# Mamba-2 decays of a hybrid decoder from two-part running sums on 32-row groups, with the first round placed ahead of the recurrence's output

## The reference, cut to what matters

```python
dt = softplus(dt_raw + dt_bias)
a = -jnp.exp(a_log)
a_dt = dt * a                                   # 8 heads, 256 tokens, never positive
a_cum = jnp.cumsum(a_dt, axis=-1)
seg = a_cum[..., :, None] - a_cum[..., None, :]
lmat = masked_exp(seg, _causal_mask(ln))        # exp of the segment sums, causal
cb = jnp.einsum('bclgn,bcsgn->bgcls', cc, bc)   # 2 groups
y_diag = jnp.einsum('bgecls,bcsgep->bclgep', cb[:, :, None] * lmat, xc)
```

## Time and profile before

| | us |
|---|---|
| median of 3 runs (lowest, highest) | 1519.15 (1518.85, 1520.54) |
| the profiled execution's own time | 1520.9 |
| its span, first to last instruction | 1518.6 |
| PE busy | 1480.4 (97%) |
| DVE busy | 1176.1 (77%) |
| ACT busy | 938.8 (62%) |
| POOL busy | 51.5 (3%) |

### The profile page before, as it was taken

One profiled execution on the slowest core, in us unless ns is written; L12 is line 12 of the kernel. 1 busy time (PEld: TensorE's weight loads), 2 busy tenths in 40 slices (PEclk: granted clock), 3 DMA queues, 4 the chain that ended last, 5 costly groups with the idle time before them and its releaser, 6 DMA issues.

```text
span 1518.6 us, 21694 instructions
## 1 busy us (share of the span) xinstructions
PE 1480.4 (97%) x8411; PEld 1288.3 (85%) x8411; DVE 1176.1 (77%) x1143; ACT 938.8 (62%) x952; POOL 51.5 (3%) x58
## 2 busy tenths in 40 slices
PE   8999999999999999999999999999999999999996
PEld 8989898999889989897888887888878888888884
DVE  6886654555447887656998998989989899898996
ACT  6655444444437654454777778777777777777773
POOL 0031000000000121000000000000000000000000
PEclk9999999999999999999999999999999999999998
DMA  7433443455546432534699998999889999999993
GB/s 307 142 137 112 149 157 139 143 191 181 185 167 219 140 112 96 185 136 166 248 361 383 346 351 343 352 378 359 342 343 351 377 362 341 361 353 373 365 361 123
DMA packets 54484, 388.51 MB, mean 256 GB/s; under 512 B 6000, under 2 KB 6256, under 8 KB 8176
## 3 DMA queue, kind: packets, MB, share of 16 engines
q1 hardware_dynamic: 53840, 384.98, 67.6%
q10 hardware_dynamic: 544, 2.10, 0.3%
HBM read 386.00 MB, written 1.05 MB: 255 GB/s over the span
## 4 chain that ended last, share of the span: by engine, by line
issue 53%; PE 44%; DVE 2%; DMA 0%; ACT 0%; POOL 0%; DVEq 0%; POOLq 0%
PE pb L1027 12%; PE pb L1029 12%; PE pb L1028 12%; PE pb L1168 1%; PE pb L1246 1%; PE pb L1266 1%; PE pb L1008 1%; DVE xTl L1589 0%; PE pb L1212 0%; DMA h<-in_x 0%; PE pb L1256 0%; PE pb L1222 0%; PE pb L1214 0%; PE pb L1223 0%; PE pb L1213 0%
## 5 line engine op out<-in xcount | busy, mean ns | idle before, releaser
L2105 DVE TENSOR_TENSOR wlo<-raw,whi 128x2048 fp32r<-128x2048 f32 x175 | 400.5, 2291 | 50.5 <-ACT whi L939 48.6
L939 ACT ACTIVATE whi<-raw 128x2048 fp32r<-128x2048 f32 x175 | 335.8, 1919 | 134.7 <-PE pb L1029 134.7
L1540 DVE TENSOR_TENSOR wlo<-raw,whi 128x2048 fp32r<-128x2048 f32 (+1 forms) x101 | 225.7, 2246 | 132.3 <-ACT whi L592 131.9
L1027 PE MATMUL pb<-whi,mTh 128*128 128x512 f32 x768 | 305.0, 397 | 4.9 <-DVE kvXr L2105 3.7
L1029 PE MATMUL pb<-whi,mTl 128*128 128x512 f32 x768 | 300.1, 391 | 0.0
L592 ACT ACTIVATE whi<-raw 128x2048 fp32r<-128x2048 f32 (+1 forms) x101 | 190.1, 1884 | 176.8 <-PE pb L1029 167.6
L1027 PE MATMUL pb<-xTh,whi 128*128 128x256 f32 x736 | 210.0, 285 | 2.0 <-DVE xTl L1577 1.2
L2105 DVE TENSOR_TENSOR kvXr<-kvX,whi 128x2048 fp32r<-128x2048 f32 x86 | 196.7, 2291 | 19.3 <-ACT whi L939 17.8
L1028 PE MATMUL pb<-xTl,whi 128*128 128x256 f32 x736 | 208.2, 283 | 0.0
L1029 PE MATMUL pb<-xTh,wlo 128*128 128x256 f32 x736 | 208.2, 283 | 0.0
L1028 PE MATMUL pb<-wlo,mTh 128*128 128x512 f32 x528 | 205.6, 389 | 0.0
(11 more groups left out here) (330 smaller groups left out, 2220.7 us busy)
## 6 DMA issues: line engine op xcount, KB each, us to landing
raw<-in_ffn_w SPq DMA_DIRECT2D x209, 1024.0 KB, 4.8
kvX<-in_ffn_w SPq DMA_DIRECT2D x88, 1024.0 KB, 4.9
raw<-in_lin_w SPq DMA_DIRECT2D x64, 1024.0 KB, 4.7
raw<-in_lin_w SPq DMA_DIRECT2D x4, 536.0 KB, 5.2
arena<-in_mem ACTq DMA_DIRECT2D x2, 1024.0 KB, 7.8
h<-in_x SPq DMA_DIRECT2D x1, 1024.0 KB, 5.1
out<-xn SPq DMA_DIRECT2D x2, 512.0 KB, 2.7
consts<-in_con SPq DMA_DIRECT2D x1, 836.0 KB, 12.8
```

What stands on the lines that cost most here:

```text
L939: nc.scalar.activation(whi[:, (MOE0 + c) % HRING, :], xraw_slots[c % XRING], ACT.Copy).then_inc(hi_ready, 1)
L1027: nc.tensor.matmul(o, lh, rh, start=first, stop=False)
L1540: V.tensor_tensor(wlo[:, m % RING, c], raw[:, m % RING, c], whi[:, m % HRING, c].bitcast(F32), ALU.subtract).then_inc(lo_ready, 1)
L2105: V.tensor_tensor(xlo_slots[c % XRING], xraw_slots[c % XRING], whi[:, (MOE0 + c) % HRING, :].bitcast(F32), ALU.subtract).then_inc(lo_ready, 1)
```

## The change

- **Running sums instead of masks.** DVE no longer builds `ABm` and `ALm`. Behind the fox maxima it cuts each token's decay into two parts, a coarse one (rounded by adding and subtracting 3072) and the rest, and writes them into columns 32 i to 32 i + 3 of `Wm`, for head i of a round. PE multiplies `Wm` with two triangular masks behind the fox transposes (four matmuls of 128 columns, bank 7): these are the sums towards the border of the two tiles. ACT makes `Qm` and `Km` of them, in which each 32-row group holds four rows in use (coarse, one, rest, one, with signs), and PE waits for them ahead of the fox output.
- **Rounds.** The segment sums of a head are then `Km` times `Qm` on the 32 rows of that head: one matmul of 256 columns and one of 128, with the four heads of a round in four row groups and four banks. DVE clamps the own-tile blocks at zero in PSUM (`nonpositive`) ahead of the exponential.
- **Order.** Round one moves ahead of the recurrence's output, which goes to the second bank of z in place of bank 7; z's activation on ACT moves ahead of the convolution's, so that this bank is free. Its exponential follows (`decays(0)`) before xk0 is copied. The B-C products now wait for that exponential in place of the recurrence's copy. xk1(0) moves ahead of round two, and xk1(1) waits for the recurrence's copy.
- **DVE's order.** The heads' squares come ahead of the B-C product; `xcd` ahead of the splits of chunks 17 and 18; then the product of round one, the clamp of round two, the split of chunk 19, and the product of round two. `ytmp` moves behind the heads' output.

```diff
+COARSE = 3.0 * 2.0 ** 10
...
+             np.concatenate([row[0] - row[2], row[1] + row[3], row[3] - row[1], row[0] + row[2]], axis=1)]
...
-        Mm = carve(8736, M2_H, 3 * P)
+        Mm = [carve(at, 4, 3 * P) for at in (14368, 8736)]
...
-        ALm = carve(14368, NT, M2_H, P)
-        ABm = carve(2560, M2_H, P)
+        Wm = carve(9760, NT, 2, P)
+        Km = carve(2560, 2, S)
+        Qm = carve(3072, 2, S)
...
+                act.wait_ge(m2_c, layer + 1)
+                units = [const("units")[:, i:i + 1] for i in range(4)]
+                sums = pb[:, 7, :].rearrange("p (r s) -> p r s", r=2)
+                nc.scalar.activation(Qm, sums, ACT.Identity, scale=units[0], bias=units[1])
+                nc.scalar.activation(Km, sums, ACT.Identity, scale=units[2], bias=units[3]).then_inc(m2_rows, 1)
...
+                projected(act, "z", layer)
+                b = bank("z", layer)
+                nc.scalar.activation(zs, pb[:, b:b + 2, 0:512], ACT.Silu).then_inc(lin_act, 1)
                 act.wait_ge(conv_ready, layer + 1)
                 nc.scalar.activation(xcv, xcv, ACT.Silu).then_inc(xcv_ready, 1)
-                take("z", layer, (zs, 0, 512, ACT.Silu, 1.0, None))
-                split_to(last_chunk(layer, "xk0") + 2)
+                after("z", layer)
+
+                def decays(r):
+
+                    act.wait_ge(m2_neg, 2 * layer + r + 1)
+                    nc.scalar.activation(Mm[r], pb[:, 4:8, 0:3 * P], ACT.Exp).then_inc(m2_e, 1)
+
+                decays(0)
+                take("xk0", layer, (tiles(kX[:, 0:4, :]), 0, 512, ACT.Copy, 1.0, None))
                 act.wait_ge(m2_t, layer + 1)
                 nc.scalar.activation(xs, pb[:, 6:8, :], ACT.Copy).then_inc(m2_xs, 1)
-                take("xk0", layer, (tiles(kX[:, 0:4, :]), 0, 512, ACT.Copy, 1.0, None))
-                for r in range(2):
-                    act.wait_ge(m2_seg, 2 * layer + r + 1)
-                    nc.scalar.activation(Mm[:, 4 * r:4 * r + 4, :], pb[:, 4:8, 0:3 * P], ACT.Exp).then_inc(m2_e, 1)
-                    if r == 1:
-                        split_to(chunk0(layer, "xk1") + HRING)
+                decays(1)
+                split_to(chunk0(layer, "xk1") + HRING)
                 take("xk1", layer, (tiles(kX[:, 4:8, :]), 0, 512, ACT.Copy, 1.0, None))
...
                 mm.then_inc(fox_pt, 1)
+                pe.wait_ge(m2_w, layer + 1)
+                for rnd in range(2):
+                    o = pb[:, 7, rnd * S:(rnd + 1) * S]
+                    nc.tensor.matmul(o[:, 0:P], Wm[:, 0, rnd, :], const("after"), start=True, stop=True)
+                    mm = nc.tensor.matmul(o[:, P:S], Wm[:, 1, rnd, :], upto, start=True, stop=True)
+                mm.then_inc(m2_c, 1)
...
+                pe.wait_ge(m2_rows, layer + 1)
                 pe.wait_ge(fox_ptc, layer + 1)
...
                 project("xk0", layer, M, (0,))
+                def segments(rnd):
+
+                    for i in range(4):
+                        r = slice(32 * i, 32 * i + 32)
+                        nc.tensor.matmul(pb[:, 4 + i, 0:2 * P], Km[r, rnd, 0:P], Qm[r, rnd, :], start=True, stop=True)
+                    for i in range(4):
+                        r = slice(32 * i, 32 * i + 32)
+                        mm = nc.tensor.matmul(pb[:, 4 + i, 2 * P:3 * P], Km[r, rnd, P:S], Qm[r, rnd, P:S], start=True,
+                                              stop=True)
+                    mm.then_inc(m2_seg, 1)
+
                 pe.wait_ge(hg_sel, (layer + 1) * (MASKED + 1))
                 pe.wait_ge(hg_wide, (layer + 1) * len(WIDE))
+                segments(0)
+                pe.wait_ge(lin_act, evac_count(("z", layer)))
                 for hd in range(HG_H):
                     v = vtok[:, :, 256 + hd * DH:256 + (hd + 1) * DH]
                     at = 4 * (hd % 2) + 2 * (hd // 2)
-                    o = pb[:, 7, :].rearrange("p (t h d) -> p t h d", t=NT, h=HG_H)
+                    o = pb[:, bank("z", layer) + 1, :].rearrange("p (t h d) -> p t h d", t=NT, h=HG_H)
                     nc.tensor.matmul(o[:, 0, hd, :], ScT[:, at, :], v[:, 0, :], start=True, stop=True)
                     nc.tensor.matmul(o[:, 1, hd, :], ScO[:, at // 2, :], v[:, 0, :], start=True, stop=False)
...
                 pe.wait_ge(xcv_ready, layer + 1)
-                pe.wait_ge(hg_ok, layer + 1)
+                pe.wait_ge(m2_e, 2 * layer + 1)
...
                 mm.then_inc(m2_t, 1)
-                pe.wait_ge(m2_a, layer + 1)
+                project("xk1", layer, M, (0,))
                 pe.wait_ge(m2_cb, layer + 1)
                 pe.wait_ge(m2_xs, layer + 1)
-                for rnd in range(2):
-                    if rnd:
-                        project("xk1", layer, M, (0,))
-                        pe.wait_ge(m2_e, 2 * layer + 1)
-                    for i in range(4):
-                        hd = 4 * rnd + i
-                        b = pb[:, 4 + i, :]
-                        nc.tensor.matmul(b[:, 0:2 * P], ALm[:, 0, hd, :], upto_ones, start=True, stop=False)
-                        nc.tensor.matmul(b[:, P:2 * P], ABm[:, hd, :], upto, start=False, stop=True)
-                        mm = nc.tensor.matmul(b[:, 2 * P:3 * P], ALm[:, 1, hd, :], upto, start=True, stop=True)
-                    mm.then_inc(m2_seg, 1)
+                segments(1)
+                pe.wait_ge(hg_ok, layer + 1)
                 project("xk1", layer, M, (1,))
                 pe.wait_ge(m2_m, 2 * layer + 2)
...
+                def pairs(ap):
+
+                    return ap.rearrange("p (r i) -> p r i", r=2).unsqueeze(3).to_broadcast([P, 2, 4, 2])
+
+                for t in range(NT):
+                    ins = V.tensor_scalar(Z12[:, t, 4:12], A12[:, t, 4:12], 2.0 * t - 1.0, COARSE, ALU.mult, ALU.add)
+                link(ins)
+                for t in range(NT):
+                    at = Wm[:, t, :, :].rearrange("p r (i x) -> p r i x", x=32)
+                    V.tensor_scalar(at[:, :, :, 0:2], pairs(Z12[:, t, 4:12]), -COARSE, None, ALU.add)
+                    ins = V.scalar_tensor_tensor(out=at[:, :, :, 2:4], in0=pairs(Z12[:, t, 4:12]), scalar=-COARSE,
+                                                 in1=pairs(A12[:, t, 4:12]), op0=ALU.add,
+                                                 op1=ALU.subtract if t else ALU.add)
+                ins.then_inc(m2_w, 1)
...
 
-                V.tensor_copy(ABm, bc(A12[:, 1, 4:12], P))
-                for t in range(NT):
-                    ins = V.tensor_tensor(ALm[:, t, :, :], const("after").unsqueeze(1).to_broadcast([P, M2_H, P]),
-                                          bc(A12[:, t, 4:12], P), ALU.mult)
-                ins.then_inc(m2_a, 1)
+                def nonpositive(rnd):
+
+                    dve.wait_ge(m2_seg, 2 * layer + rnd + 1)
+                    own = pb[:, 4:8, 0:3 * P].rearrange("p b (i s) -> p b i s", i=3)[:, :, 0:3:2, :]
+                    V.tensor_scalar(own, own, 0.0, None, ALU.min).then_inc(m2_neg, 1)
+
+                nonpositive(0)
                 dve.wait_ge(hg_o, layer + 1)
-                V.tensor_copy(xn[:, :, 256:512], pb[:, 7, :].rearrange("p (t c) -> p t c", t=NT)).then_inc(hg_ok, 1)
+                V.tensor_copy(xn[:, :, 256:512], pb[:, bank("z", layer) + 1, :].rearrange("p (t c) -> p t c", t=NT)
+                              ).then_inc(hg_ok, 1)
 
                 ss = ssq.rearrange("p (t c) -> p t c", c=10)
                 rs = rstd.rearrange("p (t c) -> p t c", c=10)
                 heads = xn[:, :, 0:512]
                 after("z", layer)
-                dve.wait_ge(m2_t, layer + 1)
-                V.tensor_tensor(CBs, pb[:, 4:6, 0:3 * P], const("m2mask").unsqueeze(1).to_broadcast([P, 2, 3 * P]),
-                                ALU.mult).then_inc(m2_cb, 1)
-                after("xk0", layer)
-                dve.wait_ge(m2_xs, layer + 1)
-                for t in range(NT):
-                    tokens = xs[:, t, :].rearrange("p (h d) -> p h d", d=DH)
-                    V.tensor_tensor(xcd[:, t, :].rearrange("p (h d) -> p h d", d=DH), tokens, bc(SP12[:, t, 4:12], DH),
-                                    ALU.mult)
-                    V.tensor_tensor(ytmp[:, t, :].rearrange("p (h d) -> p h d", d=DH), tokens,
-                                    bc(par_("m2_d", layer), DH), ALU.mult)
                 dve.wait_ge(hg_ok, layer + 1)
                 link(V.tensor_tensor(sqh, heads, heads, ALU.mult))
                 link(V.tensor_reduce(ss[:, :, 0:8], sqh.rearrange("p t (h d) -> p t h d", d=DH), AX.X, ALU.add))
                 V.tensor_scalar(ss[:, :, 0:8], ss[:, :, 0:8], 1.0 / DH, EPS, ALU.mult, ALU.add).then_inc(ss_ready, 1)
+                dve.wait_ge(m2_t, layer + 1)
+                V.tensor_tensor(CBs, pb[:, 4:6, 0:3 * P], const("m2mask").unsqueeze(1).to_broadcast([P, 2, 3 * P]),
+                                ALU.mult).then_inc(m2_cb, 1)
+                def by_heads(ap, t):
+
```

(43 more changed lines are left out.)

## The result

The changed kernel takes 1531.91 us (median of 4, 1531.35 to 1535.77) against 1519.02 (1518.85 to 1520.54): a ratio of 1.0082, 95% interval 1.0070 to 1.0094. It is 12.9 us slower, where 1.0 us slower, 1520.2, was forecast and 1524.2 was the top of the range.

The account below looks back on a forecast made before the run. TensorE (PE), busy 97% of the span, was taken to bound the kernel. Work at -0.5 us plus a clock loss of 1.5 gave +1.0 on the median 1519.15: 1520.2, range 1515.8 to 1524.2.

Parts of the forecast that it names:

- PE's work: PE's sums and rounds: 0.88 and two of 1.1 added, 6.93 and a 1.20 wait removed; 5.05 us shorter per layer.
- rival 2: Segment-sum rounds on PE: 32-row groups run one after another, 3.0 us a round, 1523.9 in all; chance 0.17.
- The chain to y: From xk0(1)'s end through ACT and DVE: y starts 19.9 us later, PE idles about 5, work gives -0.5 us.
- rival 3: Round two's clamp in PSUM on DVE costs 2.4 us, +3.4 in all, 1522.5; chance 0.10.
- Edits at nothing: Small DVE weight steps, ACT's passes over the sums, and round one's clamp and exp: all covered, costing nothing.
- Rival 1: Before y: chunk 19's split is not in the way, PE idles 0.8 us, 9 us faster, 1510; chance 0.10.
- The clock: Half clock after the idle before y: 0.75 us per layer, 1.5 in all, bounds 0 and 1.7 per layer.
- The dip agrees: Claim that the earlier trace's mid-run clock dip, priced at 1.7 us, supports the skill's advice against long idle gaps.
- the sum: Whole kernel: -0.5 for the work plus 1.5 for the clock, +1.0 us, 1520.2 against the median.

Follow-up runs that it names:

- experiment 1: Changed kernel with DVE's split of chunk 19 put back behind the product of round two: 1515.29 us, ratio 0.9963 to the kernel before.
- experiment 8: Changed kernel with round two's clamp ahead of round one's product and chunk 19's split behind both products: 1508.94 us, ratio 0.9928 to the kernel before.
- experiment 5: Changed kernel, idle kept, with the wide product xv0(0) moved ahead of y behind the same wait: 1537.63 us.
- experiments 3 to 7: DVE squarings added: kernel before 1543.81, experiment 8 1527.69; changed kernel with xv0(0) before y 1537.63, extra matmuls before y, wide 1530.61, narrow 1543.00 us.

## Why the prediction was wrong

- **PE's work:** right. Forecast 0.88 for the sums, 1.1 for a round, 5.05 us per layer in all; measured 0.91, 0.87 and 5.42 (0.91 + 1.06 - 4.95 - 2.44 = -5.42, where 1.06 is round one with the changes of form around it). The four row groups ran at once, so rival 2 is out. 12 units of 0.219 in a row are 2.63, and 2.63 / 0.87 = 3.0. The Trainium skill's 3.07 for four 32-row tiles ("TensorE: Matmul & The Clock Gate", section on packing small matmuls) agrees.
- **The chain to y:** right. Forecast 19.9 us behind xk0(1) and an idle of about 5; measured 602.33 - 582.46 = 19.87 and 4.97. The split of chunk 19 was the cause (experiment 1). The clamp took 1.23 against the 1.21 of the earlier trace rows; rival 3 is out.
- **Edits at nothing:** the small DVE steps, ACT's two passes and the early round brought no wait of PE in the new stage; of PE's waits only y's is new there. The 2.09 us at 30.7 us lie ahead of everything that the change touches in a layer.
- **Rival 1** (faster, 1510) did not happen, and was what experiment 8 then made: 1508.9.
- **The clock: the step that failed.** "I take half, 0.75 per layer, 1.5 in all, bounds 0 and 1.7 per layer." Measured 6.1 and 7.5, 13.6 in all. The price came from the earlier trace rows, one dip of 3.4 us with matmuls of 256 columns behind it, and I took its length over as it was. (Half of 1.7 is also 0.85 and not 0.75; that is 0.2 in all and changes nothing.) The length depends on what follows. Behind y's idle stand 24 products of 64 columns, and the dip lasts 13.7 and 17.1 us (in the profiles 3.4 to 6.8 where wide work follows). Why it is 13.7 in one layer and 17.1 in the other, behind the same idle, stays open. The bound was also no bound: a single case at another place in the program set both price and ceiling. The advice of the Trainium skill against idle gaps between bursts ("TensorE: Matmul & The Clock Gate", on why this matters) pointed the right way; its size had to come from these runs. "The dip agrees" claimed too much: the idles ahead of the dip of the earlier trace rows were 0.49 and 0.99 us, no long gap. Here too a half clock followed idles of 0.96 and 1.80 us, shorter than the gaps that the page warns of; where the page and these runs differ, the runs decide. With the measured price the sum would have been -0.5 + 13.6 = +13.1: 1532.1.

## What to carry to other kernels

When a change shortens the bound engine's work, the wait that appears must be priced twice: its length, and the clock behind it, read from which matmuls come next. A wait ahead of narrow matmuls cost two to three times its length here (11.0 and 12.4 us for 4.97, some 9 for 3.12), so an unavoidable wait is cheaper ahead of wide ones, if that delays nothing else (experiment 5 shows what it can delay), or filled. In a hand-ordered program, don't let an engine split or round a chunk between two steps of the chain when another engine prepares that chunk only behind the first of them.

## What the runs showed of the hardware

- A half clock that began in an idle of 3.1 to 5.2 us, or up to 1.4 us behind it, lasted 10.2 to 20.5 us with float32 matmuls of 64 columns behind the idle, and 6.8 us, part of it in the idle, with float32r matmuls of 256 or 512 columns (the change and experiments 3 to 7).
- The same narrow matmuls hold a full clock: 22 of them and y's 24 in a row ran at 1.00 (1519.52).
- An idle of 0.96 us ahead of narrow matmuls was followed by a half clock of 10.2 us in one layer of an execution and by none in the other. What decides between them stays open.
- Useless work paid: 80 wide matmuls in the two idles took 12.8 us off the kernel.
